# RWKV scan: steps of preparation staggered between the two directions, key norms over ten turns, turned operands two turns earlier

## The reference, cut to what matters

```python
w_logit = w0 + tanh(xw @ w1) @ w2
decay = exp(-exp(-softplus(-w_logit) - 0.5))
a = sigmoid(a0 + (xa @ a1) @ a2)
kk = k * k_k
kk = kk / max(norm(kk, axis=-1), 1e-12)
k_dir = k * (1 + (a - 1) * k_a)          # a, decay and k_dir are one for each direction
# step, with a_t = -kk, b_t = kk * a:
sa = einsum('bhij,bhj->bhi', s, at)
s = s * wt + sa[..., None] * bt + vt[..., None] * kt
y = einsum('bhij,bhj->bhi', s, rt)
```

## Time and profile before

| | us |
|---|---|
| median of 3 runs | 3767.67 (3767.37 to 3768.85) |
| the profiled execution | 3773.46 |
| its span | 3771.7 |
| TensorE matmul busy | 3474.8 (92%) |
| VectorE busy | 1589.3 (42%) |
| ScalarE busy | 1152.5 (31%) |
| GpSimd busy | 389.5 (10%) |
| mean granted TensorE clock | 0.958 |

### The profile page before, as it was taken

One profiled execution on the slowest core, in us unless ns is written; L12 is line 12 of the kernel. 1 busy time (PEld: TensorE's weight loads), 2 busy tenths in 40 slices (PEclk: granted clock), 3 DMA queues, 4 the chain that ended last, 5 costly groups with the idle time before them and its releaser, 6 DMA issues.

```text
span 3771.7 us, 77399 instructions
## 1 busy us (share of the span) xinstructions
PE 3474.8 (92%) x34504; PEld 2589.4 (69%) x34504; DVE 1589.3 (42%) x3134; ACT 1152.5 (31%) x2424; POOL 389.5 (10%) x606
## 2 busy tenths in 40 slices
PE   7999998999999799799999997999999899799897
PEld 3565556788888578698888886578878677453333
DVE  1254236433333543366666664333343474311112
ACT  2232123322223223255555553222243332200001
POOL 0000013100000100122222221000010200000000
PEclk9999999999999899899999998799999899799999
DMA  4283124211111110000000001222221122579997
GB/s 197 84 350 150 45 114 177 86 49 68 68 68 68 64 45 23 7 6 5 5 5 5 5 5 54 89 90 90 90 88 45 45 103 72 243 307 428 428 427 306
DMA packets 34940, 434.13 MB, mean 115 GB/s; under 512 B 4992, under 2 KB 5600, under 8 KB 9136
## 3 DMA queue, kind: packets, MB, share of 16 engines
q1 hardware_dynamic: 29664, 413.44, 27.5%
q0 software_dynamic: 4944, 15.74, 1.3%
HBM read 423.92 MB, written 5.24 MB: 114 GB/s over the span
## 4 chain that ended last, share of the span: by engine, by line
PE 79%; DMA 8%; DVE 6%; ACT 5%; issue 1%; POOL 0%; SPq 0%; DVEq 0%; ACTq 0%; POOLq 0%
PE ps L771 16%; PE ps L1937 8%; PE ps L1939 8%; PE ps L1938 8%; PE ps L2353 7%; PE ps L3694 5%; PE ps L712 5%; DMA part<-in_wu 4%; DMA part<-in_wg 3%; PE ps L695 3%; PE ps L2346 3%; PE ps L2360 2%; PE ps L1017 2%; PE ps L2468 1%; ACT L71 1%; PE ps L2459 1%
## 5 line engine op out<-in xcount | busy, mean ns | idle before, releaser
L771 PE MATMUL ps<-part 128*128 128x512 f32 (+1 forms) x3120 | 626.3, 363 | 30.8 <-DVE part L1002 11.0
L771 PEld LDWEIGHTS ps<-part 128*128 128x128 f32 x3120 | 525.2, 194 | 132.4 <-DVE part L1002 12.2
L1937 PE MATMUL ps<-part 128*128 128x512 f32 (+1 forms) x1536 | 550.2, 358 | 18.1 <-DVE part L1984 11.4
L1938 PE MATMUL ps<-part 128*128 128x512 f32 (+1 forms) x1536 | 549.5, 358 | 0.0
L1939 PE MATMUL ps<-part 128*128 128x512 f32 (+1 forms) x1536 | 549.3, 358 | 0.0
L3694 PE MATMUL ps<-part 128*64 128x512 f32 x1536 | 376.3, 614 | 35.6 <-DMA part<-in_wg 17.3
L1961 DVE TENSOR_TENSOR part<-part 128x1024 fp32r<-128x1024 f32 x128 | 158.1, 1235 | 497.6 <-ACT part L1950 497.6
L2353 PE MATMUL ps<-part 64*64 64x64 f32 x9984 | 343.4, 220 | 21.1 <-ACT part L2676 11.9
L2353 PEld LDWEIGHTS ps<-part 64*64 64x64 f32 x9984 | 317.8, 136 | 51.9 <-ACT part L2676 12.9
L1937 PEld LDWEIGHTS ps<-part 128*128 128x128 f32 x1536 | 290.3, 189 | 68.1 <-DVE part L1984 12.6
L1938 PEld LDWEIGHTS ps<-part 128*128 128x128 f32 x1536 | 290.8, 189 | 46.5
(11 more groups left out here) (410 smaller groups left out, 4685.1 us busy)
## 6 DMA issues: line engine op xcount, KB each, us to landing
part<-in_ada_w SPq DMA_DIRECT2D x36, 2048.0 KB, 8.6
part<-in_mlp_w SPq DMA_DIRECT2D x32, 2048.0 KB, 7.7
part<-in_wg SPq DMA_DIRECT2D x32, 2048.0 KB, 22.2
part<-in_wu SPq DMA_DIRECT2D x32, 2048.0 KB, 22.2
part<-in_wd SPq DMA_DIRECT2D x32, 2048.0 KB, 22.2
part<-in_b_in SPq DMA_DIRECT2D x8, 2048.0 KB, 7.8
part<-in_ab_w_in SPq DMA_DIRECT2D x7, 2048.0 KB, 7.7
part<-in_rkv SPq DMA_DIRECT2D x6, 2048.0 KB, 7.4
```

Of the source, the lines that this page charges most:

```text
L771: mm = pe.e.matmul(ps[:, j * n:j * n + n], lhs, rhs, start=k == ks[0] and i == 0, stop=k == ks[-1] and i == 2)
L1937: pe.e.matmul(ps, wh[:, k, :], hi[:, k, x0:x1], start=k == 0, stop=False)
L1938: pe.e.matmul(ps, wh[:, k, :], lo[:, k, x0:x1], start=False, stop=False)
```

## The change

It changes the turns of prep and of the keys' steps, and moves `bk` and its copy from turn 11 to turn 9 of the same unit. No operation is added or removed.

- prep, direction 0: steps 0 to 7 in turns 0, 1, 2, 4, 6, 7, 8, 10; direction 1: in turns 1, 2, 3, 5, 7, 8, 9, 11.
- keys: steps 0 to 5 in turns 0, 2, 4, 5, 8, 9.

```diff
-PREP = {1: 0, 3: 1, 4: 2, 5: 3, 6: 4, 7: 5, 8: 6, 9: 7}
+PREP = ({0: 0, 1: 1, 2: 2, 4: 3, 6: 4, 7: 5, 8: 6, 10: 7}, {1: 0, 2: 1, 3: 2, 5: 3, 7: 4, 8: 5, 9: 6, 11: 7})
+KEYS = {0: 0, 2: 1, 4: 2, 5: 3, 8: 4, 9: 5}
@@ rw_turns
-            if (n + 2) % 3 == 0 and (n + 2) // 3 < 8 and turn <= 5:
-                yield "kk", turn, (n + 2) // 3
+            if (n + 2) % 3 == 0 and (n + 2) // 3 < 8 and turn in KEYS:
+                yield "kk", KEYS[turn], (n + 2) // 3
@@
-                if 0 <= n + 1 < UNITS and turn in PREP:
-                    yield "prep", PREP[turn], Unit(K, d, n + 1)
+                if 0 <= n + 1 < UNITS and turn in PREP[d]:
+                    yield "prep", PREP[d][turn], Unit(K, d, n + 1)
@@ rw_pe, solve
                     gram(u, ps, u.bb, u.ops[:, 3:4, :]).then_inc(*pe.up(("br", *u.key)))
+            if turn == 9:
                 ps = K.bank("bk", *u.key)
@@ rw_act, solve
-            if turn == 11:
+            if turn == 9:
                 s.wait_ge(K.at("bk", *u.key))
```

## The result

| | before | after |
|---|---|---|
| median (3 runs and 4) | 3767.7 us | 3795.9 us (3794.1 to 3801.3) |
| ratio to before, 95% interval | | 1.0068 (1.0056 to 1.0080) |
| profiled execution, its span | 3773.5, 3771.7 us | 3796.5, 3794.7 us |
| TensorE matmul busy | 3474.8 us | 3500.1 us |
| VectorE, ScalarE busy | 1589.3, 1152.5 us | 1578.2, 1153.8 us |

The change makes the kernel 28 us slower by the medians (23 us by the two profiled executions). By the interval of the ratio it is 21 to 30 us. TensorE has the same number of matmuls and is busy for 25.3 us more, which is a little more than the two profiled executions differ by: this change didn't add waiting, it added busy time on the engine that is the bound.

What follows compares the result with a forecast made beforehand. TensorE alone bounds A and C; B also has stops. Terms 16.5 (loras in A and C) + 0.5 (B) + 2 (unit 1) + 0.5 (unit 22) = 19.5, say +19 us: median 3767.7 to 3787, range 3766 to 3807.

Steps and rivals of the forecast that it cites:

- A: Scan units with n a multiple of 3, bound by TensorE alone: 26.5 us before, forecast near 27.6.
- C: Scan units with n = 3m+2, bound by TensorE alone: 28.6 us before, forecast near 29.7.
- the second rival: A lone lora costs half of the pair, 0.2 us a unit: about 3770 us, no change; chance 0.12.
- A lone lora costs as much as the pair: Start of each unit: splitting the loras adds a TensorE block, UU 1.1 us later; 16.5 us over 15 units of A and C.
- no gain, no loss in A and C: zero: `bk` and its copies in turn 9: zero; some 0.3 us a unit if its cover of VectorE's mask were gone.
- B: Scan units with n = 3m+1, holding next keys' norms and last y's finish: 40.2 us before, forecast within 1.5 of that.
- The late last step of prep: Direction 1's last preparation step, in turn 11 on VectorE ahead of `gram` 1: counted zero, up to 0.3 us a unit.
- The first rival: No stop in turn 9 on turned v's copy, clock stays up: some 16 us faster, 3752 us; chance 0.10.
- Unit 1 and unit 22: Units like B, but 1 lacks y's finish and 22 lacks keys: forecast +2 and +0.5 us.
- The first unit's preparation lies ahead of all: Start of the scan: the first unit's preparation was taken to cost nothing.
- as before, one fall: Granted clock in B: one fall after the longest stop, as before, so no change in its cost.
- The third rival: Second clock fall in B (1.6 us, 7 times) and late preparation holding `gram` (0.3 in 23 units): 3805 us; chance 0.18.

Runs made afterwards that it cites:

- the kernel with one table load: Kernel before, loras paired in turn 1, prep respread to turn 10, keys' ln and exp behind y's in turn 6, turned v copied in turn 8: 3728.0 us, ratio 0.9900.

## Why the prediction held, point by point

It forecast 3787 us; the median is 3795.9. The sign and both mechanisms were as forecast; the sum came out 9 us short, term by term. Luck had a part in the count. The 15 units of lora in A and C take in unit 23, which prepares nothing and has no lora, and leave out unit 0, which prepares unit 1 and has one; the two slips cancel in the count, though unit 0 costs 3.0 us and not 1.1. And the second rival adds up to some 3767, not to its "about 3770".

- **A lone lora costs as much as the pair: shown.** 1.1 us a unit was forecast. Moved by itself it costs 1.19 in A and in C, and with each engine's chain left alone again 1.19. The argument from one row carried it: 376 ns at 64 rows against 379 at 128. The Trainium skill, TensorEngine Tiling (Array Packing), Key Properties, has it that different tiles work in parallel and that a change of mode drains the engine; the runs agree with the first, since the pair takes 1.07 us and one alone 1.06. The second could be no more than the 0.13 us by which 1.19 exceeds 1.06, which no run takes apart from the issue. The second rival (the lone lora is cheap) falls.
- **A: 27.6 forecast, 27.93 measured.** The step that failed is "no gain, no loss in A and C: zero" for `bk`. The prediction had named the cover, VectorE's mask of PX, under `bk`'s *new* place, and asked whether it would be late there. It didn't ask what `bk` had covered in its *old* place: the copy of UU ahead of y in turn 11. Moved alone it costs 0.43 us in A, nothing in B and C. The prediction's "if that cover were gone some 0.3 us a unit" was near the price for it. In the whole change A's excess over the lora is 0.24 (1.43 less 1.19), and the kernel with the pair back in turn 1 shows the same 0.25. The stagger of the midpoints gives back the rest. Before, VectorE has the midpoints of direction 0 in turn 4 between the two directions' adds, and from the 32 matmuls of `X add` in turn 5 (2054.26 in unit 15) to ZZ (2055.35) it is 1.09 us; after, with the midpoints in turns 2 and 3, it is 0.93 (2071.43 to 2072.36). It is 1.09 or 1.10 in A and C of the kernels with only the lora moved, with only the keys moved and with the loras apart, which leave the midpoints in turn 4; and the kernel with one table load, which has them in turn 3, has A and C 0.2 shorter than before. So A is 1.19 + 0.43 - 0.16 = 1.46, against 1.43 measured.
- **C: 29.7 forecast, 29.73 measured.** The unit grew by 1.02, which is the lora's 1.19 less the 0.16 that the midpoints give back here too. The late last step of prep, bounded at up to 0.3 us, is 0.6 when the lone lora isn't there, and nothing in the change but for unit 23, since the lora covers it.
- **B: within 1.5 of 40.2 forecast, 40.4 measured in the mean.** Its terms held one by one: the stop in turn 5 on the keys' maximum was forecast at 0.7 and is 0.61, that of turn 8 at 1.2 and is 0.96, that of turn 9 at 3.5 and is 3.33. That the last is the ring of banks is shown by turned v moved later: the stop goes, though ScalarE has the same work. The first rival (no stop in turn 9) fails by the same row. The four loads lie within 9.2 us.
- **Unit 1 and unit 22:** +2 and +0.5 forecast, +1.5 and +0.1 measured.
- **Unit 0: forecast at nothing, +3.0 measured.** "The first unit's preparation lies ahead of all" is the step that failed: that holds for the preparation of unit 0, but unit 1 is prepared in unit 0, with a split lora as everywhere. And the scan begins behind 11 us of idle time of TensorE, with the granted clock at 0.50. The start of unit 0 after:

```profile
1579.86 1.22 PE L2378 MATMUL ps<-part 64*128 64x256 f32 x2
1580.87 1.06 PE L2379 MATMUL ps<-part 64*128 64x256 f32 x2
1581.86 1.44 PE L2347 MATMUL ps<-part 64*64 64x64 f32 x22
```

  A lone lora takes 2.00 us at this clock, and so does the second (1583.76 to 1585.76); before, the pair took 1.35, with the clock rising in it (1579.67 to 1581.02). From the first `gram` to the end of the second lora it is 7.81 us after and 4.96 before: 2.85 of the 3.0. The clock also stays low for longer; the row of the unit after, and of the kernel before:

```profile
1577.70:1604.60 26.90, 25.91 (x616) 23.49 (x616) 15.31 (x42) 9.58 (x24) 6.43 (x12) 0.79 0.02 3
```

```profile
1576.00:1600.00 24.00, 22.53 (x620) 21.12 (x622) 16.86 (x45) 8.85 (x23) 7.54 (x12) 0.91 0.01 4
```

  Unit 0 is long in all three kernels that have a lora between its two `gram` (26.9, and 27.7 with only the lora of direction 0 moved and with turned v late), and 22.4 to 24.5 us in the others. The kernel with the loras apart behind both `gram` is no exception: what parts them there is RH, which unit 0 doesn't have, so in unit 0 they are neighbours. Why the clock rises later wasn't tested.
- **The clock inside B** was forecast "as before, one fall": right in the mean. By unit it is not one number. Units 7 and 16 of the kernel after (13 stands above):

```profile
1792.80:1831.55 38.75, 33.66 (x865) 28.94 (x863) 24.47 (x60) 22.77 (x55) 10.09 (x22) 1.00 0.03 7
2085.70:2127.05 41.35, 36.26 (x864) 31.54 (x862) 24.46 (x60) 22.76 (x55) 10.08 (x22) 0.92 0.03 6
```

  The idle time is the same in all of them (5.1 us); TensorE's busy time is 33.7, 35.3 and 36.3 us. The third rival priced a second fall at 1.6 us a unit. A longer fall is there in some units (+1.0 over the usual one), balanced by a unit without any.

In short, the profiled execution was forecast at 3792.5 and took 3796.5. Of these 4 us, unit 0 is 3.0 and A 2.4 (10.1 against 7 times 1.1); C, B with units 1 and 22, and what lies around the scan are 1.4 less together. The other 5 us of the median are no step of the change: the profiled execution of before lay 5.8 us above its median, that of after 0.6, and the prediction had carried the 5.8 over.

Two clear misses were in the experiments. The pair in turn 0 with its tanh was expected to cost nothing and cost 35 us, by ScalarE's queue. And the keys' steps alone were expected to gain over 20 us and gained nothing. The layout by hand of B had counted ScalarE's queue in turns 6 to 9 with care and VectorE's in turn 4 not at all. The stop grew where nobody had looked: behind the midpoints, and in the unit after.

## What to carry to other kernels

Two small products on opposite halves of the array are worth one product as long as they stand next to each other in the queue; moving one of them away adds a full product to the bound engine without adding an instruction, and the counts of instructions and the waits won't show it, only the busy time will. When a step is moved, ask of its old place what it had been hiding, as carefully as you ask of its new one what hides it: three moves here (`bk`, the pair, turned v) each uncovered a wait for a copy on another engine. And before spreading work over more turns, look for what makes it long: here four table loads a period. Two of them went by putting the two users of one table side by side, and 15 of the 39 us gained hang on that; the other 24 came from a layout that also spread the steps, but with VectorE's turn 4 and the copies that TensorE waits for in mind, where the first spreading gave nothing.

## What the runs showed of the hardware

- Two fp32 matmuls of 256 columns at 64 rows take as long alone as with their twin on the other 64 rows: 1.06 us for 4 of them, 1.07 us for 8, from the first row until the next product starts.
- The same stop doesn't always lower the clock. A stop of 3.3 us in turn 9 left the granted clock of the unit at 1.00 in unit 7, and brought it to 0.96 and 0.92 in others: 38.75, 40.4 and 41.35 us for one sequence of instructions. Units of one kind are to be compared only at the same granted clock.
- A table load behind other work costs its own 1.28 us and 0.02 beside it: the load at 2014.90 and the next ln at 2016.20 are 1.30 us apart. The Trainium skill, ScalarE: Activation LUTs, What ACT_TABLE_LOAD costs, has some 2.66 us for each switch with its drain; no load in the scan shows the second half of that: in all 31 of them the next activation starts 1.29 or 1.30 us behind the load.
